# RWKV-7 triangular solve in a two-layer decoder step: one pass over eight heads in place of two passes over four

## The reference

```python
def step(S, inp):
    r_t, d_t, k_t, v_t, kk_t, b_t = inp
    sa = jnp.einsum('bhij,bhj->bhi', S, -kk_t)
    S = S * d_t[:, :, None, :] + sa[..., None] * b_t[:, :, None, :] + v_t[..., None] * k_t[:, :, None, :]
    return S, jnp.einsum('bhij,bhj->bhi', S, r_t)
...
S, y = lax.scan(step, s0.astype(f32), xs)
```

## Time and profile before

| | us |
|---|---|
| median of 3 runs (lowest to highest) | 3399.21 (3396.51 to 3399.39) |
| the profiled execution | 3401.5 |
| its span, first to last instruction | 3399.6 |
| PE busy (share of the span) | 3272.0 (96%) |
| DVE busy | 1711.3 (50%) |
| ACT busy | 1208.5 (36%) |
| mean granted PE clock (1 is full speed) | 0.979 |

### The profile page before, as it was taken

The page is one execution under the profiler, slowest core; times in us unless marked ns, Lnnn a source line. Parts: engine busy times, 40 slices in busy tenths (PEclk is TensorE's granted clock), DMA queues, the critical chain, the costliest instruction groups (busy, mean ns, idle before and its releaser), DMA issues.

```text
span 3399.6 us, 60962 instructions
## 1 busy us (share of the span) xinstructions
PE 3272.0 (96%) x25078; PEld 3074.4 (90%) x25078; DVE 1711.3 (50%) x2269; ACT 1208.5 (36%) x1607; POOL 91.9 (3%) x209
## 2 busy tenths in 40 slices
PE   7999888999999999999999988889999999999998
PEld 6999755699999999999999986557999999999998
DVE  5455572355555454454545664714555544545544
ACT  3332256433322222222434313654422323323234
POOL 1000011000000000000000000100000000000000
PEclk9999889999999999999999998999999999999999
DMA  6552036765555554554564610577655545545454
GB/s 196 164 135 65 2 132 234 258 151 150 150 150 140 159 148 138 160 148 140 152 190 136 137 27 2 191 278 201 148 149 151 149 140 164 149 136 161 137 146 132
DMA packets 848704, 501.17 MB, mean 147 GB/s; under 512 B 96608, under 2 KB 823152, under 8 KB 848112
## 3 DMA queue, kind: packets, MB, share of 16 engines
q1 hardware_dynamic: 848108, 499.01, 51.7%
q10 hardware_dynamic: 452, 0.11, 0.0%
HBM read 485.71 MB, written 13.37 MB: 147 GB/s over the span
## 4 chain that ended last, share of the span: by engine, by line
PE 91%; DVE 4%; ACT 2%; issue 1%; DMA 1%; ACTq 0%; SPq 0%; DVEq 0%
PE PS L1435 87%; PE PS L1436 4%; ACT ktr L884 1%; ACT psm L855 0%; DVE psm L1303 0%; DVE wl L962 0%; ACT ppt L866 0%; DVE nm L1305 0%; ACT wh L641 0%; DVE S0T L1255 0%; DMA sink<-in_c_sink 0%; DVE rt L1080 0%; DMA raw<-in_w_out 0%; DVE WT L1183 0%; DMA raw<-in_w_in 0%
## 5 line engine op out<-in xcount | busy, mean ns | idle before, releaser
L641 ACT ACTIVATE wh<-raw 128x2048 fp32r<-128x2048 f32 (+1 forms) x408 | 711.7, 1744 | 1235.7 <-PE PS L1435 1214.2
L962 DVE TENSOR_TENSOR wl<-raw,wh 128x2048 fp32r<-128x2048 f32 (+1 forms) x408 | 848.9, 2081 | 400.2 <-ACT wh L641 399.6
L1435 PE MATMUL PS<-fh,wh 128*128 128x320 f32 x2816 | 870.6, 309 | 0.0
L1435 PE MATMUL PS<-fh,wl 128*128 128x320 f32 x2816 | 870.1, 309 | 0.0
L1435 PE MATMUL PS<-fl,wh 128*128 128x320 f32 x2816 | 870.1, 309 | 0.0
L1435 PEld LDWEIGHTS PS<-fh,wh 128*128 128x128 f32 x2816 | 528.5, 188 | 0.2
L1435 PEld LDWEIGHTS PS<-fl,wh 128*128 128x128 f32 x2816 | 528.5, 188 | 0.2
L1435 PEld LDWEIGHTS PS<-fh,wl 128*128 128x128 f32 x2816 | 528.5, 188 | 0.0
L1435 PE MATMUL PS<-hh,wh 128*128 128x320 f32 (+2 forms) x1696 | 521.3, 314 | 4.8 <-DVE wl L962 4.8
L1435 PE MATMUL PS<-hh,wl 128*128 128x320 f32 (+2 forms) x1696 | 513.5, 309 | 0.0
L1435 PE MATMUL PS<-hl,wh 128*128 128x320 f32 x1664 | 510.5, 310 | 0.0
(11 more groups left out here) (329 smaller groups left out, 2711.4 us busy)
## 6 DMA issues: line engine op xcount, KB each, us to landing
raw<-in_w_gate SPq DMA_DIRECT2D x88, 1024.0 KB, 5.6
raw<-in_w_up SPq DMA_DIRECT2D x88, 1024.0 KB, 5.6
raw<-in_w_down SPq DMA_DIRECT2D x128, 704.0 KB, 4.8
raw<-in_w_in SPq DMA_DIRECT2D x56, 1024.0 KB, 5.6
cK<-in_cache_a_k SPq DMA_DIRECT2D x80, 512.0 KB, 6.5
cV<-in_cache_a_v SPq DMA_DIRECT2D x60, 512.0 KB, 8.8
raw<-in_w_in SPq DMA_DIRECT2D x32, 512.0 KB, 5.3
raw<-in_w_out SPq DMA_DIRECT2D x32, 512.0 KB, 4.5
```

The costliest lines, as they stand in the source:

```text
L641: act.activation(wh[j][:, 0:kts], raw[j][:, 0:kts], ACT.Copy).then_inc(sem["wh"], 1)
L962: tt(wl[j][:, 0:kts], raw[j][:, 0:kts], wh[j][:, 0:kts].bitcast(F32), ALU.subtract).then_inc(sem["wl"], 1)
L1435: mm = lambda out, lhsT, rhs, start=True, stop=True: pe.matmul(out, lhsT, rhs, start=start, stop=stop, skip_group_check=True)
```

## The change

All eight heads go through each step together: one ZZ copy of 512 columns, one subtraction of 512 columns for `TT` and one for `WT`, one mask of 512 columns for `ET`, and one wait for each on PE. T uses bank 0 and W bank 2, whole; Z alternates between banks 6 and 7 from level to level. POOL's first mask of a round becomes one instruction of 512 columns. The matmuls themselves stay, 16 for a step in rounds 0 and 1 and 8 in round 2.

```diff
-                    for hf in range(2):
-                        m = C(f"lev{LEVELS[0]}", nt).unsqueeze(1).broadcast_to([nt, 4, HD])
-                        x, y = (z[0:nt, hf * 256:(hf + 1) * 256].rearrange("p (h t) -> p h t", h=4) for z in (MT, ET))
-                        pool.tensor_tensor(y, x, m, ALU.mult).then_inc(sem["et0"], 1)
+                    m = C(f"lev{LEVELS[0]}", nt).unsqueeze(1).broadcast_to([nt, 8, HD])
+                    x, y = (z[0:nt].rearrange("p (h t) -> p h t", h=8) for z in (MT, ET))
+                    pool.tensor_tensor(y, x, m, ALU.mult).then_inc(sem["et0"], 1)
...
-                        for hf in range(2):
-                            take("Z")
-                            act.activation(ZZ[0:nt, hf * 256:(hf + 1) * 256], PS[0:nt, ZB[hf], 0:256], ACT.Copy).then_inc(sem["Zc"], 1)
+                        take("Z")
+                        act.activation(ZZ[0:nt], PS[0:nt, ZB[i % 2], :], ACT.Copy).then_inc(sem["Zc"], 1)
...
                     for i, size in enumerate(levels):
                         last = i == len(levels) - 1
+                        zs[0] += 1
                         if not last:
-                            for hf in range(2):
-                                zs[0] += 1
-                                dve.wait_ge(sem["Z"], zs[0])
-                                corner(levels[i + 1], hf)
-                        else:
-                            zs[0] += 2
-                        for hf in range(2):
-                            if not last:
-                                take("TZ")
-                                done(tt(quad(TT, hf), quad(TT, hf), qbank(TB[hf]), ALU.subtract), "TT")
-                            take("WZ")
-                            done(tt(quad(WT, hf), quad(WT, hf), qbank(WB[hf]), ALU.subtract), "TW")
+                            dve.wait_ge(sem["Z"], zs[0])
+                            corner(levels[i + 1])
+                            take("TZ")
+                            done(tt(each(TT), each(TT), each(PS[:, TB[0], :]), ALU.subtract), "TT")
+                        take("WZ")
+                        done(tt(each(WT), each(WT), each(PS[:, WB[0], :]), ALU.subtract), "TW")
...
+                        if i:
+                            take("et")
+                            take("TT")
+                        else:
+                            take("et0")
+                            take("E1")
+                        per_head(ZB[i % 2], ET, TT, range(8)).then_inc(sem["Z"], 1)
+                        take("Zc")
+                        if i:
+                            take("TW")
+                        else:
+                            take("NT")
+                            take("RB")
+                        if size != levels[-1]:
+                            per_head(TB[0], WT, ZZ, range(8)).then_inc(sem["TZ"], 1)
+                        per_head(WB[0], ZZ, WT, range(8)).then_inc(sem["WZ"], 1)
```

More of the change, by code:

```diff
@@ L1191, in rwkv, with corner @@
                     levels = LEVELS if tau < 2 else LEVELS[:2]
[L1192 to L1197, removed]
+                    each = lambda x: x[0:nt, 0:512].rearrange("p (h t) -> p h t", h=8)
+                    def corner(size):
+                        m = C(f"lev{size}", nt).unsqueeze(1).broadcast_to([nt, 8, HD])
+                        done(tt(each(ET), each(MT), m, ALU.mult), "et")
                     for i, size in enumerate(levels):
                         last = i == len(levels) - 1
+                        zs[0] += 1
                         if not last:
-                            for hf in range(2):
-                                zs[0] += 1
-                                dve.wait_ge(sem["Z"], zs[0])
-                                corner(levels[i + 1], hf)
-                        else:
-                            zs[0] += 2
-                        for hf in range(2):
-                            if not last:
-                                take("TZ")
-                                done(tt(quad(TT, hf), quad(TT, hf), qbank(TB[hf]), ALU.subtract), "TT")
-                            take("WZ")
-                            done(tt(quad(WT, hf), quad(WT, hf), qbank(WB[hf]), ALU.subtract), "TW")
+                            dve.wait_ge(sem["Z"], zs[0])
[4 more added lines that the diff above has]
+                        done(tt(each(WT), each(WT), each(PS[:, WB[0], :]), ALU.subtract), "TW")
                     take("NV")
@@ L1630, in rwkv @@
                     for i, size in enumerate(levels):
-                        for hf in range(2):
-                            hs = range(4 * hf, 4 * hf + 4)
-                            if i:
-                                take("et")
-                                take("TT")
-                            else:
-                                take("et0")
-                                if not hf:
-                                    take("E1")
-                            per_head(ZB[hf], ET, TT, hs).then_inc(sem["Z"], 1)
-                        for hf in range(2):
-                            hs = range(4 * hf, 4 * hf + 4)
-                            take("Zc")
-                            if i:
-                                take("TW")
-                            elif not hf:
-                                take("NT")
-                                take("RB")
-                            if size != levels[-1]:
-                                per_head(TB[hf], WT, ZZ, hs).then_inc(sem["TZ"], 1)
-                            per_head(WB[hf], ZZ, WT, hs).then_inc(sem["WZ"], 1)
+                        if i:
[14 more added lines that the diff above has]
+                        per_head(WB[0], ZZ, WT, range(8)).then_inc(sem["WZ"], 1)
                         if tau == 1 and i < 4:
@@ L1661, in rwkv @@
                                 a.then_inc(sem["st"], 1)
-                    take("TW", 2)
+                    take("TW")
                     if tau == 1:
```

## The result

The changed kernel is slower: 3422.25 us, median of 4 runs (3416.28 to 3425.34), against 3397.86 for the kernel before beside it (3391.45 to 3399.39). The ratio is 1.0075, with a 95% interval from 1.0058 to 1.0091. The predicted 3416 (3407 to 3432) had the sign, the mechanism and, in its range, the size; the delay itself was predicted as 17 us and measured as 20 to 31.

What follows compares the result with a forecast made beforehand. PE was taken as the bound, all but full in a pipeline of two halves. Rounds cost 4.2 + 3.0 + 1.3 = 8.5 us a layer, 17 in two: 3401.5 + 17 = 3418.5, median 2.3 below, 3416 (3407 to 3432).

Steps and rivals of the forecast that it cites:

- A steady level: One solve level, T to next T: 3.86 us in round 0 (0.82 more), 4.89 in round 1 (0.69 more).
- The last W: A round's last level, from W to the next step: 2.00 us in place of 1.74, 0.26 more.
- The start of round 0: First T of round 0: 1.0 us late (0.2 to 1.2), released by ACT, with POOL's mask taken as 2.26.
- called covered for rounds 1 and 2: First T there still released by `RBm`; in round 1 PE's 2.01 us wait covers longer Z, copy and later mask.
- The rounds together: Added time of the three solve rounds: 4.2, 3.0 and 1.3 us, 8.5 a layer, 17 in two layers.
- Round 2: PE at about half speed: single ZZ copy and last W make next step 1.3 us later; first level unchanged.
- The clock in steady levels: Granted clock stays at full in the solves' steady levels, though PE pauses about 1 us in each.
- Rival 1: Clock falls or stays down within the solves: 3432 us in its smaller form, 3452 in its larger; chance 0.15.
- Rival 2: Clock stops falling at the starts of rounds: 3397 us if every fall went, 3410 for rounds 0 and 1; chance 0.06.
- I let all of it through: Behind the solves, through next round and attention: nothing absorbs the delay, so all 17 us reach the total.

Runs made afterwards that it cites:

- the products that nobody reads: Matmuls of constants, result unused, put into PE's waits at each round's start: changed kernel with them 3412.12 us, kernel before with them 3397.28 us.

## Why the prediction was right, step by step

- **A steady level** of round 0: predicted 3.86 us, measured 3.93. The one link that was off is the handover from DVE to PE, 0.12 us in place of 0.05, 0.2 us in all for a round. Round 1: 4.89 predicted, 4.88 measured. Four steps in halves make PE the bound; whole, the loop through DVE and ACT is. The runs with one half of the change show that Z and its copy carry most of it: 0.67 of the 0.89 us of a level. This was shown.
- **The last W**: 2.00 predicted, 2.01 measured.
- **The start of round 0** was mis-sized, and the round's sum came out by luck. Predicted: T 1.0 us late, released by ACT, after a mask of 2.26. Measured: 0.53 late (5.27 us behind the first mask on `TT`, before 4.74), released by `RBm`, with ACT's copy 0.02 us ahead of it; in the second trace of the changed kernel ACT did release it, once. The term that was off is POOL's price, 1.67 us: put into the forecast's own sum it makes T 0.42 late. The other 0.11 is a cost that I had missed: DVE's product on `WT`, 1.63 us in place of 1.09, in front of `NTm` and `RBm`. What I had called covered for rounds 1 and 2 costs 0.13 there by the same route. The first level then took 5.17, 0.6 more than before where I had 0.5. The 0.5 too much at the start and the 0.3 too little in the levels nearly cancel.
- **The rounds together**, from the first mask to the copy of NV, differ between the two pairs of traces, since the clock does. Predicted for a layer are 4.2, 3.0 and 1.3 us for rounds 0, 1 and 2. The first pair gives 4.1, 3.1 and 1.9 in layer 0 and 3.8, 3.1 and 1.8 in layer 1; the second pair 5.6, 1.4 and 0.6, and 4.0, 1.5 and 1.4. Round 1's agreement in the first pair holds for a clock that falls in both kernels' first levels. In the second trace of the changed kernel it did not fall there, and the round was 1.6 to 1.7 us shorter.
- **Round 2** in layer 0 of the first pair: from the last W on the 0.37 of the forecast measured 0.32. Up to the last W it was 1.41 more (5.50 us from 414.22 to 419.72, before 4.09 from 406.93 to 411.02) in place of 0.89: here the clock fell during T, where before it fell two pieces later, and I had put the first level at nothing. Another 0.13 came from the start, as in round 1.
- **The clock in steady levels**: it stayed at 1.00 with PE busy for 1.31 and 1.98 of 2.00 us. Rival 1 did not come about. The rule of the Trainium skill that I had weighed (TensorE: Matmul & The Clock Gate, "A second HAM failure mode: psum-queue depth-cycling") would, as I had read it, have had it swing; the trace does not agree for pauses of 0.69 us a level.
- **The clock at the starts** moved the time of both kernels. The stretch at half speed hangs on PE's wait there (no first level of rounds 0 and 1 has one with the products that nobody reads), but the wait does not bring it every time. Those products are worth 9.6 us at the median in the changed kernel, 1.3 in the kernel before. Rival 2 had the mechanism; the change kept the four falls in one trace and lost three of them in the other.
- **"I let all of it through"** held for the solves: 17.7 us in one pair of traces and 14.0 in the other, against 17. What was missed is outside the loop: 1.8 us in the load of `w_out`, on which the chain does wait behind the solves, and a mean granted clock that is lower by 0.0021, by the estimate above up to 7.6 us. Nothing in the forecast had the clock fall more often than before. Which part of the distance from 17 to the measured 20 to 31 stands where is not shown.

## What to carry to other kernels

Two halves in flight are worth their extra instructions when PE's work on one half covers the copy and the subtraction of the other: write down the loop from T to T with each link's duration, once whole and once in halves, and compare it with PE's own issue time. Wider instructions were cheaper by the column here on every engine (0.69 against 2 x 0.42, 0.60 against 2 x 0.38, 1.67 against 2.26) and the kernel lost, since a level in halves had waited for PE and not for them. With halves, check that every engine takes them in the same order: the order that matched on PE and DVE made a level of round 0 as short as PE's 96 rows. Whether a few microseconds in such a loop show in the total depends on the clock as well: compare the mean granted clock of many runs before a small difference is put down to the loop.

## What the runs showed of the hardware

- A DVE product with both operands in SBUF that starts while POOL's mask of 512 columns runs ends 0.54 to 0.55 us after that mask, in all 12 places of the two traces of the changed kernel. In round 0 it ended at 314.54 after 314.00, in round 1 at 360.21 after 359.66, in round 2 at 411.32 after 410.78; it took 1.63, 1.23 and 1.22 us for the 0.69 of the same form elsewhere. DVE products from PSUM beside POOL kept their 0.69. The start of round 1:

```profile
358.39 1.27 POOL L583 TENSOR_TENSOR ET<-MT,con 128x512 f32<-128x512 f32 x1 [44.39 <-ACT MT L800]
...
358.98 1.23 DVE L1179 TENSOR_TENSOR TT<-TT,con 128x512 f32<-128x512 f32 x1
```

- It goes the other way too. POOL's mask of 512 columns takes 1.26 to 1.27 us where it starts beside a DVE product from PSUM, and 1.67 in round 0, where a DVE product with both operands in SBUF (312.19) is under way when it starts; it then ends 1.12 us behind that product. The masks of 256 columns of the kernel before show the same: 0.72 to 0.73 us alone, 1.13 and 1.17 in round 0, each 0.58 behind the end of such a product. The 2.26 us from which I had priced the wide mask held two of these waits, and one wide mask pays only one.
- The Trainium skill (SBUF — State Buffer, "SBUF: two separate sides") says that a DVE instruction with two SBUF inputs and a GpSimd one that reads SBUF lock each other out for a whole instruction. The traces agree, in both directions, and the price is up to 0.94 us on an engine that was not changed.
- The same kernel's solves differ by up to 7 us between two executions (277.0 and 270.3), with the granted clock at 0.50 for 72.6 us of them in one and 55.7 in the other: it falls at other moments behind the same waits. A single trace is no measure of a few microseconds there.
